# Expert jobs of at most 96 tokens: rounds over the last three k tiles, one bias load in place of four, and an earlier bias load for the first 97-to-128-token job

## What is computed

```python
logits = h @ w_router + b_router              # 32 experts
top_vals, top_idx = lax.top_k(logits, 4)      # each token goes to 4 experts
gates = softmax(top_vals)
# per expert e, for its tokens xb = h[toks]:
hid = xb @ w1[e] + b1[e]                      # 1024 -> 2048
x_glu, x_lin = hid[..., ::2], hid[..., 1::2]
act = min(x_glu, 7) * sigmoid(1.702 * min(x_glu, 7)) * (clip(x_lin, -7, 7) + 1)
yb = (act @ w2[e] + b2[e]) * gate             # 1024 -> 1024
out[toks] += yb
```

## Time and profile before

| what | value |
|---|---|
| time of three runs | 1971.86, 1971.12, 1969.52 us; median 1971.12 |
| the profiled execution: its own time, and its span | 1971.53 us, 1969.7 us |
| PE busy | 1910.2 us (97%) |
| DVE, ACT, POOL busy | 66%, 21%, 12% |
| mean granted clock of TensorE | 0.989 of full speed |
| mean DMA traffic | 253 GB/s |
| slim jobs, narrow jobs on PE | from 1272.3 us; from 1488.7 us to the end |

### The profile page before, as it was taken

One profiled execution on the slowest core, in us unless ns is written; L12 is line 12 of the kernel. 1 busy time (PEld: TensorE's weight loads), 2 busy tenths in 40 slices (PEclk: granted clock), 3 DMA queues, 4 the chain that ended last, 5 costly groups with the idle time before them and its releaser, 6 DMA issues.

```text
span 1969.7 us, 33296 instructions
## 1 busy us (share of the span) xinstructions
PE 1910.2 (97%) x12224; PEld 1398.8 (71%) x12224; DVE 1303.0 (66%) x3759; ACT 411.8 (21%) x910; POOL 235.6 (12%) x317
## 2 busy tenths in 40 slices
PE   7999999997999999999999999999998999999996
PEld 5677777774999999999999999834333444444442
DVE  2787778774377777775666666645355767777665
ACT  1233332222121122222222222223221100001100
POOL 1212222221010111111111111110100000000000
PEclk8999999998999999999999999999999999999998
DMA  9411100113966778788888989999999999999992
GB/s 311 113 43 43 43 18 35 32 33 144 339 207 228 246 261 269 245 282 278 289 285 283 307 300 304 316 368 381 360 368 382 382 375 356 369 369 367 360 360 72
DMA packets 207682, 498.39 MB, mean 253 GB/s; under 512 B 7716, under 2 KB 14928, under 8 KB 200080
## 3 DMA queue, kind: packets, MB, share of 16 engines
q1 hardware_dynamic: 194016, 449.43, 63.7%
q0 software_dynamic: 11312, 39.85, 8.2%
q10 hardware_dynamic: 2304, 8.39, 1.0%
HBM read 470.24 MB, written 27.41 MB: 253 GB/s over the span
## 4 chain that ended last, share of the span: by engine, by line
issue 40%; PE 29%; DMA 5%; POOL 1%; DVE 1%; POOLq 0%; ACT 0%; DVEq 0%; ACTq 0%
PE ps_unit L1885 29%; DMA out_dram<-y_rows,idx_cur 4%; POOL x_got L1378 1%; DMA x_got<-h_rows,idx_next 0%; PE ps_list L1857 0%; POOL carrier L1374 0%; POOL out_dram L1435 0%; POOLq L1096 0%; POOLq L1290 0%; DVE match L1562 0%; DVE reached L1610 0%; POOL out_dram L1390 0%; POOLq L1426 0%; POOLq L1265 0%; DVE xT L1684 0%
## 5 line engine op out<-in xcount | busy, mean ns | idle before, releaser
L1885 PE MATMUL ps_unit<-xT,w_slot 128*128 128x136 f32 (+6 forms) x3840 | 521.5, 298 | 1.6 <-DVE xT L1684 1.6
L1885 PEld LDWEIGHTS ps_unit<-xT,w_slot 128*128 128x128 f32 x3840 | 516.6, 196 | 2.0 <-issue 2.0
L1915 PE MATMUL ps_unit<-w_slot,xT 128*128 128x512 f32 x704 | 306.7, 594 | 0.0
L1279 DVE STREAM_TRANSPOSE xT<-x_got 32x256 f32<-32x256 f32 x644 | 280.5, 436 | 12.1 <-DMA x_got<-h_rows,idx_next 3.7
L1885 PE MATMUL ps_unit<-act_T,w_slot 128*128 128x136 f32 (+6 forms) x1920 | 261.6, 298 | 0.1
L1885 PEld LDWEIGHTS ps_unit<-act_T,w_slot 128*128 128x128 f32 x1920 | 257.9, 190 | 2.2 <-DVE act_T L1659 1.5
L1915 PEld LDWEIGHTS ps_unit<-w_slot,xT 128*128 128x128 f32 x704 | 132.8, 190 | 163.0 <-issue 163.0
L1675 DVE STREAM_TRANSPOSE y_rows<-yT 32x256 f32<-32x256 f32 x372 | 162.1, 436 | 55.0 <-ACT yT L1481 50.1
L928 PE MATMUL ps_c<-hT,w_in_sb 128*128 128x128 f32 x1536 | 182.1, 279 | 4.3 <-DMA w_in_sb<-in_w_in_dram 4.3
L928 PEld LDWEIGHTS ps_c<-hT,w_in_sb 128*128 128x128 f32 x1536 | 177.3, 194 | 9.6 <-DMA w_in_sb<-in_w_in_dram 5.2
L1374 POOL TENSOR_TENSOR carrier<-carrier 128x1 f32<-128x1 f32 x64 | 14.5, 227 | 1319.1 <-issue 610.8
(11 more groups left out here) (294 smaller groups left out, 1790.5 us busy)
## 6 DMA issues: line engine op xcount, KB each, us to landing
w_slot<-in_w_dram SPq DMA_DIRECT2D x192, 2048.0 KB, 12.1
b_row<-in_b_dram SPq DMA_DIRECT2D x11, 1024.0 KB, 12.9
w_in_sb<-in_w_in_dram SPq DMA_DIRECT2D x6, 1024.0 KB, 12.0
b_row<-in_b_dram SPq DMA_DIRECT2D x11, 512.0 KB, 15.1
x_in<-in_x_dram SPq DMA_DIRECT2D x8, 512.0 KB, 3.5
x_res<-in_x_dram SPq DMA_DIRECT2D x8, 512.0 KB, 4.7
out_dram<-x ACTq DMA_DIRECT2D x8, 512.0 KB, 5.1
h_rows<-h ACTq DMA_DIRECT2D x8, 512.0 KB, 3.1
```

Of the source, the lines that this page charges most:

```text
L1279: last = nc.vector.transpose(out[c * Q:(c + 1) * Q, :, tokens], rows.rearrange("p (k c j) -> p k c j", c=P // Q, j=Q)[:, :, c, :])
L1885: last = pe.matmul(ps_unit[p % RING][:, u, 0:n], w, moving[:, k, 0:n], start=(k == 0), stop=(k == KD - 1))
L1915: last = pe.matmul(ps_hid[c], xT[:, k, 0:P], w_slot[:, c, k, :], start=(k == 0), stop=(k == KD - 1))
```

## The change

It has five parts. (1) Layer one of a slim job goes k tile by k tile only up to k = 4; the last three k tiles go t by t ("rounds"), and the turn of tile t - 1 stands behind the round of tile t. The third turn stands behind the first half of layer two for t = 0. Turns 1 and 2 now wait until ACT has read the turn before (`slim_actT`). Buffer 2 is handed back at the last round's k = 5 and not at k = 5 of the common part. (2) ACT reads the third turn before it waits for the layer-two bias. (3) One bias load per slim job for layer one in place of four. (4) The first narrow job's layer-one bias is issued behind its first weight buffer and not behind its fourth. (5) The loop over narrow jobs on SP starts at 1, with the first job ahead of it.

```diff
+SPLIT = 5
...
-        b1_spread = event("b1_spread", 64)
+        b1_spread = event("b1_spread", 16)
...
-                    for g in range(W1_LOADS):
-                        src = b1[0, bass.ds(e, 1), g * LW:(g + 1) * LW].rearrange("o f -> (o f)")
-                        sp.dma_start(b1_row[g * TILE:(g + 1) * TILE, 0:LW], src.partition_broadcast(TILE)).then_inc(b1_spread.sem, 16)
+                    src = b1[0, bass.ds(e, 1), :].rearrange("o (g f) -> (o g) f", g=W1_LOADS)
+                    sp.dma_start(b1_row[:, 0:LW], src.unsqueeze(1).broadcast_to([W1_LOADS, TILE, LW])).then_inc(b1_spread.sem, 16)
...
-                with sp.Fori(0, narrow_jobs) as t:
+                def load_narrow(t, first_bias_behind):
...
-                        if i == W1_LOADS - 1:
+                        if i == first_bias_behind:
...
+                load_narrow(0, 0)
+                with sp.If(narrow_jobs > 1):
+                    with sp.Fori(1, narrow_jobs) as t:
+                        load_narrow(t, W1_LOADS - 1)
...
                     slim_read_act(s, 1)
+                    slim_read_act(s, 2)
                     wait(act, b2_spread, s)
                     wait(act, cur_ready, q)
                     nc.scalar.activation(b2_row[0:SLIM, :], b2_row[0:SLIM, :], ACT.Copy,
                                          scale=gate_cur[0:SLIM, 0:1]).then_inc(slim_b2.sem, 1)
-                    slim_read_act(s, 2)
...
                 wait_round(pe, slim_rows, s, t)
+                if t > 0:
+                    wait_round(pe, slim_actT, s, t - 1)
...
-                for k in range(KD - 2):
+                for k in range(SPLIT):
...
-                    if k % 2 == 1:
+                    if k in (1, 3):
                         last.then_inc(w_used[k // 2].sem, 1)
...
                 for t in range(TILES):
-                    for k in (KD - 2, KD - 1):
+                    for k in range(SPLIT, KD):
                         last = slim_first(t, k)
+                        if t == TILES - 1 and k == 5:
+                            last.then_inc(w_used[2].sem, 1)
                     last.then_inc(round_done.sem if t < TILES - 1 else w_used[W1_LOADS - 1].sem, 1)
-                for t in range(TILES):
-                    slim_turn(s, t)
+                    if t > 0:
+                        slim_turn(s, t - 1)
+                slim_second(s, q, 0, range(0, 4))
+                slim_turn(s, 2)
+                for t in range(1, TILES):
                     slim_second(s, q, t, range(0, 4))
```

## The result

The changed kernel takes 1981.95 us (median of 6 runs, 1980.46 to 1983.76), the kernel before 1971.84 (6 runs beside them, 1969.52 to 1973.99). The ratio is 1.0056 with a 95% interval of 1.0046 to 1.0066: slower by 10 us between the medians and 11 by the ratio, where 5.5 were forecast. The profiled execution took 1982.54 us, its span is 1980.8.

What follows compares the result with a forecast made beforehand. Late DMA landings, with the queue at 38.3 us per slim job against PE's 34.82, were taken as the ceiling. - 6.0 + 0.8 + 12.0 - 1.3 = + 5.5 us gave 1976.6 us, range 1962.5 to 1982.5.

Steps and rivals of the forecast that it cites:

- Four engines: Merged slim bias load: its source's 4 pieces confine it to four DMA engines, 32 packets of 2 KB each.
- 100 ns a packet, 12.0 us: DMA queue: 24 more packets on the busiest engines, 2.4 us per job, 12.0 us lost over five slim bias loads.
- Half of the 2.7 us between engines as a credit, - 1.3,: Merged load: if its four engines are not those ending last, part of the delay is hidden; 1.3 us taken off.
- The ceiling, - 6.0: Second narrow job: its layer-one bias, landing at 1541.8, ends the job no sooner than 1572.3; at most 6.0 us won.
- The clock behind the stop, + 0.8: Second narrow job: PE's stop of some 3 us may cost clock, 0 to 1.7 us; 0.8 taken.
- Rounds and turns, 1.1 us per job: Slim jobs on PE: three stops of 1.69 us filled with work, less about 0.6; 1.1 us per job, 5.5 for five.
- ACT's third turn: Last two slim jobs: copying it ahead of the layer-two bias wait takes away 4.4 us of stops and 1.3 of slow matmuls.
- the first narrow bias early: First narrow job: bias ahead of buffers 1 to 3 takes away PE's 4.29 us stop and 1.7 us of slow matmuls.
- A: Rival, merged load: all 16 engines carry it, the queue loses less than now; 1961.9 us (1958 to 1966); chance 0.21.
- B: Rival, merged load: four engines, but cheap, being ahead, packets at 84 ns; 1971.5 us (1968 to 1974); chance 0.28.
- C: Rival, DMA queue: it does not bind, PE's gains arrive whole, 17.2 us; 1953.9 us; chance 0.05.

Runs made afterwards that it cites:

- the queue relieved and the bias in halves: New order, slim layer-one bias loaded for the first slim job alone (others reuse it, computation incomplete), narrow bias in two halves, against the kernel before: 1952.38 us, ratio 0.9901.

## Why the prediction was right in its direction and short by half

The time lies inside the range (up to 1982.5), on the side to which 0.46 was given, by the mechanism given. The size was off: 1976.6 was forecast, 5.4 us too little. In the profiled executions the third narrow job's start was to be 1572.3 + 0.8 + 12.0 - 1.3 = 1583.8, and is 1589.23. By the prediction's steps:

- **Four engines.** Right: 60 small packets fewer per job, and eight, four and two engines delay the bias in step. The Trainium skill, page "DMA: Bandwidth & Descriptors", section "Rules for kernel authors", confines a load to at most c engines where its outermost dimension is c and c is below 16; the three variants agree with it (32, 4 and 4 small packets per job for outermost counts of 8, 4 and 2 in four, one and two loads). The same section of the Trainium skill advises to coalesce small transfers; for one load whose outermost count is 128 this case agrees, 5.5 us faster than four, with the reservation above on its source. What the change merged was the form that loses the engines.
- **100 ns a packet, 12.0 us.** Right in size: 12.1 us between the changed kernel's bias (1556.89) and the same kernel's with four loads (1544.76). **Half of the 2.7 us between engines as a credit, - 1.3,** was wrong: nothing of it shows. That is 1.4 of the 5.4 us.
- **The ceiling, - 6.0.** This is the step that failed most. The mechanism was right: the second narrow bias sets the end of that job, and with halves in its place the gain appears. Its height was not. I took 1541.8 for its landing whatever else moved, "out of a queue that was full throughout"; with four loads and the new order it lands at 1544.7, 2.9 us later, although it is issued at 1525.5, where it was 1525.3. The step left out the scatter of the first narrow job's results (`out_dram<-y_rows`), which POOL issues and which shares the DMA engines. That job now ends earlier, so its scatter is issued at 1528.81, 16 us ahead of the bias's landing, and not at 1537.97, 4 us ahead. Between the bias's issue and its landing the kernel before moved 6.47 MB in 16.5 us, none of it for POOL; with four loads it is 7.13 MB in 19.2 us, 0.52 MB of it the scatter's. An estimate from these: 0.66 MB more at 392 GB/s is 1.7 us, and 371 GB/s in place of 392 for the 7.13 MB is 1.0. With the first narrow bias put back (1971.69 us) the scatter is issued at 1537.12, and the second bias lands 16.5 us after its issue, as before; so the late landing came with the earlier place of the first narrow bias, by which that job ends earlier, and not with the rounds in the slim jobs. No run moves the scatter alone: that it is the cause is read from the traces.
- **The clock behind the stop, + 0.8.** I took half of what the first narrow job had lost. The changed kernel lost as much as that job: from the third chunk to the job's end it took 12.2 us (1576.99 to 1589.23), not 11.2, at a granted clock of 0.86 of 2.4 GHz; with four loads it was 13.6 at 0.78. That is the last 1.0 us. In the rows shown, the matmuls behind PE's stops of 3.4 to 5.4 us are slower than their like.
- **Rounds and turns, 1.1 us per job.** 1.4: the starts are 33.4 us apart. With four loads the first two narrow jobs start at 1484.68 and 1527.43, where 1483.9 and 1526.6 were forecast. In the changed kernel it made no difference, since the queue held PE from the fourth slim job on, one job earlier than I had said.
- **ACT's third turn, and the first narrow bias early.** Both took away the stops that they were said to. The bias was worth little in the time, as the ceiling had it: putting it back costs 1.6 us (1971.69 against 1970.13). ACT's turn was not tried by itself.
- **The rivals.** A, all 16 engines, was priced at 1961.9. Its nearest kernel is the one load of 128 copies: 1964.65. B and C fall. C's number, PE's gains in whole, was 1953.9; with the queue relieved and the bias in halves it is 1952.38.

The rows behind the sentences on clock and throughput are stretches of the changed kernel, of the one with four loads (two stretches), and of the kernel before, in this order (columns as in the earlier trace rows):

```profile
1576.90:1589.30 12.40, 12.31 (x27) 5.49 (x28) 9.70 (x23) 3.12 (x4) 0.00 (x0) 0.86 1.00 365
```

```profile
1520.00:1540.00 20.00, 20.00 (x48) 8.86 (x47) 6.26 (x20) 1.75 (x2) 1.83 (x2) 1.00 1.05 369
...
1564.80:1578.50 13.70, 13.63 (x27) 6.10 (x28) 9.69 (x23) 3.12 (x4) 0.00 (x0) 0.78 1.05 392
```

```profile
1520.00:1540.00 20.00, 15.71 (x35) 6.95 (x35) 16.25 (x50) 3.12 (x4) 1.83 (x2) 0.91 1.04 393
```

The dip as the scatter passes, with four loads and then in the kernel before (same columns), and what the queues moved between the second narrow bias's issue and landing (packets, MB, share; q1 is SP's queue, q0 POOL's), in the kernel before and then with four loads:

```profile
1533.50:1537.50 4.00, 4.00 (x11) 1.84 (x10) 0.00 (x0) 0.00 (x0) 0.00 (x0) 1.00 1.05 273
...
1543.00:1547.00 4.00, 4.00 (x11) 1.82 (x10) 2.78 (x9) 0.42 (x1) 0.00 (x0) 1.00 1.06 275
```

```profile
q1 hardware_dynamic: 2836, 6.47, 104.0%
...
q1 hardware_dynamic: 2901, 6.60, 90.7%
q0 software_dynamic: 144, 0.52, 13.7%
```

## What to carry to other kernels

Before merging DMAs, look at the outermost count of the source: the small packets per load (16 or fewer) tell from the profile's page how many engines carry it, and a load on four engines is charged to every load behind it in the queue. When a gain is capped by one late landing, don't take that landing from the old trace unchanged: ask which transfers of other engines will now come ahead of it. And price the clock loss behind the stop in full. A cap found this way is often the better thing to change: one bias load in two halves, each issued earlier, was worth 6 to 8 us in each version tried, with the new order or without.

## What the runs showed of the hardware that was not expected

- Four loads of 32 partitions cost more than one of 128 partitions that writes the same bytes in as many packets of 2 KB: 5.5 us in six jobs (its source is one piece in place of four). Leaving the four out altogether for five jobs is worth 11.9 us for 1.3 MB, some 9 us per MB, where 1 MB at the 388 GB/s of the earlier trace rows takes 2.7.
- Two loads issued one behind the other, of two outermost pieces each, share the same two engines rather than taking four (1998.85 us against 1981.95 for one load of four pieces).
- Spreading a load over eight engines instead of sixteen gave times from 1974.10 to 1980.85, a wider spread than the changed kernel's 1980.46 to 1983.76; why stays open.
- As a scatter of 0.5 MB passes, some 5 to 9 us after its issue, the rate of all queues falls from about 390 to 273 GB/s for 4 us (275 in the kernel before, where it passes later). By the estimate above, a load behind it in full queues lands later by more than the scatter's own bytes take.
